# A third set of residual tiles in a hybrid decoder block: x loaded one block ahead, the final norm and its stores spread over the next feed-forward, and tiles shared to make the room

## The reference, cut to what matters

```python
u = rms_norm(h, norm_mix_g) @ w_in                  # 1024 -> 2576
c_val, c_gate, q, k, v, g, gate_lr = split(u)
y_conv = swish(layer_norm(depthwise_conv31(c_val * sigmoid(c_gate))))
y_gla = rms_norm_per_head(gated_linear_attention(q, k, v, gate_lr)) * silu(g)
h = h + concat(y_conv, y_gla) @ w_out               # 1024 -> 1024
h = h + (silu(rms_norm(h) @ w_gate) * (rms_norm(h) @ w_up)) @ w_down   # 2816 wide
out = rms_norm(h, norm_final_g)                     # the meta positions are dropped
```

## Time and profile before

| | us |
|---|---|
| median of 3 runs | 1633.14 |
| the three runs | 1630.55 to 1643.51 |
| the profiled execution's own time | 1627.47 |
| its span on core 4, the slowest | 1625.9 |
| spans of the other cores | 1613.7 to 1622.6 |

### The profile page before, as it was taken

One profiled execution on the slowest core, in us unless ns is written; L12 is line 12 of the kernel. 1 busy time (PEld: TensorE's weight loads), 2 busy tenths in 40 slices (PEclk: granted clock), 3 DMA queues, 4 the chain that ended last, 5 costly groups with the idle time before them and its releaser, 6 DMA issues.

```text
span 1625.9 us, 26606 instructions; the slowest of 8 cores (1613.7 to 1625.9 us)
## 1 busy us (share of the span) xinstructions
PE 1473.5 (91%) x7992; PEld 676.4 (42%) x8066; DVE 810.4 (50%) x1833; ACT 513.8 (32%) x808; POOL 190.8 (12%) x221
## 2 busy tenths in 40 slices
PE   2766999988999979999999988999899999999995
PEld 2333444433444434443444433444344434444442
DVE  5256436644366542754437553566427544475523
ACT  3354243222342224413162222522244131622111
POOL 1050114100040001300040000400013000400000
PEclk9887999999999999999999999999999999999998
DMA  9991899988635875367653776437853676537651
GB/s 211 249 224 52 191 261 200 216 240 222 148 135 165 240 191 159 126 189 242 160 168 123 202 223 161 151 130 218 248 159 125 186 246 161 167 132 193 199 164 65
DMA packets 144171, 294.45 MB, mean 181 GB/s; under 512 B 63264, under 2 KB 80032, under 8 KB 144032
## 3 DMA queue, kind: packets, MB, share of 16 engines
q1 hardware_dynamic: 85008, 253.82, 48.9%
q0 software_dynamic: 7056, 25.23, 9.8%
q10 hardware_dynamic: 51968, 13.70, 5.8%
HBM read 245.70 MB, written 41.94 MB: 177 GB/s over the span
## 4 chain that ended last, share of the span: by engine, by line
PE 71%; DMA 12%; DVE 6%; issue 5%; ACT 2%; ACTq 2%; SPq 2%; POOL 1%; DVEq 0%; POOLq 0%
PE ps L605 48%; PE ps L1146 17%; DMA xT<-xn_tm 5%; DMA wring<-wsc 3%; PE ps L767 2%; DMA wsc<-wring 2%; SPq L714 1%; DVE xn_tm L581 1%; PE ps L674 1%; ACTq L599 1%; ACTq L714 1%; DMA h_2<-xin 1%; DMA gng<-gla_norm_g 1%; DMA wring<-wpack 1%; DVE ftmp L1130 1%
## 5 line engine op out<-in xcount | busy, mean ns | idle before, releaser
L605 PE MATMUL ps<-x2T,wring 128*128 128x512 bf16 x2816 | 639.5, 385 | 38.8 <-DMA wring<-wsc 20.1
L605 PEld LDWEIGHTS ps<-x2T,wring 128*128 128x128 bf16 x2816 | 273.4, 99 | 392.7 <-issue 85.1
L1146 PE MATMUL ps<-wring,actT 128*128 128x512 bf16 x1368 | 312.8, 380 | 5.4 <-DMA wring<-wpack 3.3
L1130 DVE SCALAR_TENSOR_TENSOR ftmp<-ftmp,ps 128x512 f32<-128x512 f32 x176 | 120.1, 685 | 209.2 <-ACT ftmp L1129 206.7
L1129 ACT ACTIVATE ftmp<-ps 128x512 f32<-128x512 f32 x176 | 103.9, 594 | 361.1 <-PE ps L605 255.2
L1146 PEld LDWEIGHTS ps<-wring,actT 128*128 128x128 bf16 x1408 | 136.8, 98 | 163.5 <-issue 5.7
L605 PE MATMUL ps<-xT,wring 128*128 128x512 bf16 x768 | 173.0, 381 | 19.5 <-DMA xT<-xn_tm 10.2
L983 POOL TENSOR_TENSOR Rbd<-S,emid 64x256 bf16<-64x256 f32 x64 | 45.2, 705 | 909.9 <-ACT emid L817 851.3
L1132 DVE SCALAR_TENSOR_TENSOR actT<-ftmp,ps 128x512 bf16<-128x512 f32 x176 | 119.3, 685 | 46.4 <-PE ps L605 39.4
L605 PEld LDWEIGHTS ps<-xT,wring 128*128 128x128 bf16 x768 | 74.5, 98 | 113.7 <-issue 27.7
L605 PE MATMUL ps<-wring,yT 128*128 128x512 bf16 x503 | 116.8, 380 | 1.7 <-DVE sto L551 0.9
(11 more groups left out here) (191 smaller groups left out, 1260.6 us busy)
## 6 DMA issues: line engine op xcount, KB each, us to landing
wring<-wsc SPq DMA_DIRECT2D x336, 512.0 KB, 4.6
wring<-wpack POOLq DMA_DIRECT2D x48, 512.0 KB, 10.6
wsc<-wring SPq DMA_DIRECT2D x48, 512.0 KB, 10.2
rep<-vT SPq DMA_DIRECT2D x240, 67.5 KB, 2.8
h_0<-xin SPq DMA_DIRECT2D x8, 512.0 KB, 9.2
h_1<-xin SPq DMA_DIRECT2D x8, 512.0 KB, 10.2
h_2<-xin SPq DMA_DIRECT2D x8, 512.0 KB, 10.1
h_3<-xin SPq DMA_DIRECT2D x8, 512.0 KB, 10.9
```

The costliest lines, as they stand in the source:

```text
L605: ins = e.matmul(pt_ap, lhsT=lhs(kc), rhs=rhs(kc), start=(kc == 0), stop=(kc == KC - 1))
L1130: P.add("dve", lambda e: e.scalar_tensor_tensor(out=th[:], in0=th[:], scalar=1.0, in1=pg[:], op0=ALU.add, op1=ALU.mult), R=[Bpg, Bth], W=[ ...
L1146: ins = e.matmul(ps[t][:], lhsT=actT[:, j, t * 128:(t + 1) * 128], rhs=wd3[:, j - j0, :], start=(j == 0), stop=(j == NJ - 1))
```

## The change

The residual has three sets of tiles, chosen by `b % 3`. Four things follow from that, and several tiles are given up or shared to make the room.

- The x of block b+2 is loaded during FFN b, one tile behind each of the units j = 14, 16, 18 and 20. It goes into the set from which the result of block b-1 was stored in the same FFN. The x of block 1 is loaded during mixer 0, as soon as `xT` of block 0 is complete.
- The final norm of block b-1 is done during FFN b: one square-and-sum on ScalarE behind each of the units j = 0 to 3, the four row scales together at j = 5, and one scaling on VectorE with its store at j = 5, 7, 9 and 11. The last block keeps its old ending.
- The merged mixer is spread from 0% instead of 10% of the FFN.
- The four silu gates come right after q instead of among the output tiles, in block 0 too, where they stood between v and the conv. They are held in `spb` and `csb`, the decay tiles that k and q have read by then. The two small operations on the decay that followed the state product move into the decay step (`el`, `dec`).
- The conv result and the attention result are written into `xT` instead of `yT`. The attention tiles before their transpose are written into `k_tm` instead of `y_tm`. The low-rank gate's tile is one of `mtmp`, of which there are two instead of three. The starting state of a sequence is kept in memory (`s0_d`) instead of a tile.

```diff
+NH = 3
...
-SPREAD = (0.1, 0.85)
+SPREAD = (0.0, 0.85)
...
+    s0_d = nc.dram_tensor("s0", [128, 256], F32, kind="Internal").ap()
...
-        h = [[sb(f"h{s_}_{t}", [128, D]) for t in range(NT)] for s_ in range(2)]
+        h = [[sb(f"h{s_}_{t}", [128, D]) for t in range(NT)] for s_ in range(NH)]
...
-        yT = sb("yT", [128, KC, T], BF16)
...
-        sg = [sb(f"sg{i}", [128, 512]) for i in range(2)]
-        lrT = sg[0]
...
-        S0 = sb("S0", [128, 2, 128])
+        el = sb("el", [128, 2, NT])
...
-        y_tm = [sb(f"y_tm{i}", [128, 512], BF16) for i in range(2)]
+        y_tm = [k_tm[:, 2 * i:2 * i + 2].rearrange("p a b n -> p (a b n)") for i in range(2)]
...
-        mtmp = [sb(f"mtmp{i}", [128, T]) for i in range(3)]
+        mtmp = [sb(f"mtmp{i}", [128, T]) for i in range(2)]
...
+            blocks = [(s_i * seqlen + b * T, b == 0) for s_i in range(nseq) for b in range(nblk_seq)]
+            nb = len(blocks)
+
+            def load_x(b, t, after):
+                P.add("sp", lambda e: e.dma_start(out=h[b % NH][t][:], in_=xin[blocks[b][0] + t * 128:blocks[b][0] + (t + 1) * 128, :]),
+                      R=after, W=[Bh[b % NH][t]], dkey=f"h{b % NH}_{t}")
+
+            def mixer(bi, first, meta):
+                hs = bi % NH
...
-                    if load:
-                        for t in range(NT):
-                            P.add("sp", lambda e, t=t: e.dma_start(out=h[hs][t][:], in_=xin[row0 + t * 128:row0 + (t + 1) * 128, :]),
-                                  R=[Bact[2 * t + 1]] if bi > 1 else [Bvtm[t]], W=[Bh[hs][t]], dkey=f"h{hs}_{t}")
                     if first and not meta:
-                        P.add("pool", lambda e: e.tensor_copy(out=S[:, s0], in_=S0[:]), R=[BS0], W=[BS[s0]])
+                        P.add("sp", lambda e: e.dma_start(out=S[:, s0].rearrange("p a n -> p (a n)"), in_=s0_d), R=[BS0], W=[BS[s0]], dkey="s0l")
...
+                    lrT, Blr = mtm()
...
+                        if bi == 0 and nb > 1:
+                            load_x(1, t, [BxT[3]])
                         v_tile(lambda kc: xT[:, t, kc, :], [BxT[t]], v_tm[:, t, :], Bvtm[t])
                         if t == NT - 1:
                             wdone(int(bi == 0), 2)
-
-                if bi == 0:
-                    for t in range(NT):
-                        @unit(1.8)
-                        def _(t=t):
-                            gate_tile(t)
...
+                    def decay_main():
+                        decay(spb[:], Bsp, csb[:], Bcs, NT, 0)
+                        em2 = emid[:].rearrange("p (a t) -> p a t", t=NT)
+                        P.add("dve", lambda e: e.tensor_copy(out=el[:], in_=csb[:].rearrange("p a (t n) -> p a t n", n=128)[:, :, :, 127]),
+                              R=Bcs, W=[Bel])
+                        P.add("dve", lambda e: e.tensor_tensor(out=dec[:], in0=em2, in1=el[:], op=ALU.mult), R=[Bemid, Bel], W=[Bdec])
+                    stt["decay"] = decay_main
...
-                        P.add("pool", lambda e: e.tensor_copy(out=S0[:], in_=S[:, s0]), R=[BS[s0]], W=[BS0])
+                        P.add("sp", lambda e: e.dma_start(out=s0_d, in_=S[:, s0].rearrange("p a n -> p (a n)")), R=[BS[s0]], W=[BS0], dkey="s0s")
...
+                for t in range(NT):
+                    @unit(1.8)
+                    def _(t=t):
+                        gate_tile(t)
...
-                    P.add("dve", lambda e: e.scalar_tensor_tensor(out=yT[:, c, :], in0=yth[c], scalar=1.0, in1=y, op0=ALU.add,
-                                                                  op1=ALU.mult), R=[Bysq[c], Bycv[c]], W=[ByTc[c]])
+                    P.add("dve", lambda e: e.scalar_tensor_tensor(out=xT[:, :, c, :], in0=yth[c].rearrange("p (t n) -> p t n", t=NT), scalar=1.0,
+                                                                  in1=y.rearrange("p (t n) -> p t n", t=NT), op0=ALU.add, op1=ALU.mult),
+                          R=[Bysq[c], Bycv[c]], W=BxT)
...
-                    if bi == 0:
-                        return carve(10 + 2 * t, 2, F32), [Bact[10 + 2 * t], Bact[11 + 2 * t]]
-                    return sg[t % 2][:], [Bsg[t % 2]]
+                    return (spb[:, t, :], [Bsp[t]]) if t < 2 else (csb[:, t - 2, :], [Bcs[t - 2]])
...
-                    P.add("act", lambda e: e.activation(out=yT[:, 4:8, t * 128:(t + 1) * 128], in_=ptb, func=AF.Copy,
-                                                        scale=gng[:, 0:1]), R=[Bpt, Bc], W=[ByTg[t]])
+                    P.add("pe", ytr, R=[Bktm[i], Bident], W=[Bpt])
+                    P.add("act", lambda e: e.activation(out=xT[:, t, 4:8, :], in_=ptb, func=AF.Copy,
+                                                        scale=gng[:, 0:1]), R=[Bpt, Bc], W=[BxT[t]])
...
-                    if bi > 0:
-                        gate_tile(0)
                     ln_apply(3)
-
-                if bi > 0:
-                    @unit(1.8)
-                    def _():
-                        gate_tile(1)
...
-                    if t + 2 < NT and bi > 0:
-                        @unit(1.8)
-                        def _(t=t):
-                            gate_tile(t + 2)
...
-                            P.add("pe", mm8(pt[:], lambda kc: yT[:, kc, t * 128:(t + 1) * 128], lambda kc: ws[kc // 4][:, kc % 4, :]),
-                                  R=[B0, B1, ByTg[t]] + ByTc, W=[Bpt])
+                            P.add("pe", mm8(pt[:], lambda kc: xT[:, t, kc, :], lambda kc: ws[kc // 4][:, kc % 4, :]),
+                                  R=[B0, B1, BxT[t]], W=[Bpt])
...
-            def ffn(hs, orow0, last):
+            def stat(b, t):
+                i = nxt("xn", 2)
+                ht, Bht = h[b % NH][t], Bh[b % NH][t]
+                P.add("act", lambda e: e.activation(out=xn_tm[i][:], in_=ht[:], func=AF.Square, accum_out=stf[:, 0, t:t + 1]),
+                      R=[Bht], W=[Bxn[i], Bstf[t]])
+
+            def finish(b, t0, t1, n):
+
+                if n:
+                    newton_row([stf[:, k, t0:t0 + n] for k in range(6)], Bstf[t0:t0 + n], 1.0 / D, RMS_EPS)
+                for t in range(t0, t1):
+                    ht, Bht = h[b % NH][t], Bh[b % NH][t]
+                    P.add("dve", lambda e, t=t, ht=ht: e.scalar_tensor_tensor(
+                        out=ht[:], in0=ht[:], scalar=stf[:, 2, t:t + 1], in1=gfin[:], op0=ALU.mult, op1=ALU.mult),
+                        R=[Bht, Bstf[t], Bgain[id(gfin)]], W=[Bht])
+                    P.add("sp", lambda e, t=t, ht=ht: e.dma_start(out=out[blocks[b][0] + t * 128:blocks[b][0] + (t + 1) * 128, :], in_=ht[:]),
+                          R=[Bht], dkey=f"h{b % NH}_{t}")
+
+            def ffn(b, last):
...
+                        if b > 0 and j < 12:
+                            if j < NT:
+                                stat(b - 1, j)
+                            elif j % 2 == 1:
+                                finish(b - 1, j // 2 - 2, j // 2 - 1, NT if j == 5 else 0)
+                        if b + 2 < nb and j >= 14 and j % 2 == 0:
+                            load_x(b + 2, (j - 14) // 2, [Bact[j]])
...
-                def stat(t):
-                    i = nxt("xn", 2)
-                    P.add("act", lambda e: e.activation(out=xn_tm[i][:], in_=h[hs][t][:], func=AF.Square, accum_out=stf[:, 0, t:t + 1]),
-                          R=[Bh[hs][t]], W=[Bxn[i], Bstf[t]])
...
-                def final():
-                    for t in range(NT):
-                        stat(t)
-                    finish(0, NT)
...
-                        stat(t)
-                        finish(t, t + 1)
-                units.append((19.0, down_last) if last else (0.0, final))
+                        stat(b, t)
+                        finish(b, t, t + 1, 1)
+                if last:
+                    units.append((19.0, down_last))
...
-                f = ffn(b % 2, blocks[b][0], b == nb - 1)
+                f = ffn(b, b == nb - 1)
                 m = mix[b + 1] if b + 1 < nb else []
                 plan += merge(f, m, *SPREAD) if m else [fn for _, fn in f]
```

More of the change, by code:

```diff
@@ L356, in build @@
             P = Prog()
-            Bh = [[Buf(f"h{s_}_{t}") for t in range(NT)] for s_ in range(2)]
+            Bh = [[Buf(f"h{s_}_{t}") for t in range(NT)] for s_ in range(NH)]
             Bxn = [Buf(f"xn{i}") for i in range(3)]
@@ L364, in build @@
             Bx2T = [Buf(f"x2T{t}") for t in range(NT)]
-            ByTc = [Buf(f"yTc{c}") for c in range(4)]
-            ByTg = [Buf(f"yTg{t}") for t in range(NT)]
             BvT = [Buf(f"vT{c}") for c in range(4)]
@@ L373, in build @@
             Bsp = [Buf(f"sp{hp}") for hp in range(2)]
-            Bcs = Buf("cs")
+            Bcs = [Buf(f"cs{hp}") for hp in range(2)]
+            Bel = Buf("el")
             Bmid = Buf("mid")
@@ L378, in build @@
             Bk = [Buf(f"k{hp}") for hp in range(2)]
-            Bktm = Buf("ktm")
+            Bktm = [Buf(f"ktm{i}") for i in range(2)]
             Bvtm = [Buf(f"vtm{t}") for t in range(NT)]
```

(28 more changed lines are left out.)

41 lines of the change are left out of this document (12 added, 29 removed).

## The result

The changed kernel takes 1687.35 us (median of 4 runs, 1678.11 to 1694.09) against 1632.39 for the kernel before: a ratio of 1.0318, 95% interval 1.0241 to 1.0395. It is 3.2% slower. The prediction of 1595 us and its range up to 1625 were wrong. The profiled execution took 1678.11 us, with a span of 1676.2.

A forecast was written before the change was run, and what follows sets the result against it. TensorE, 91% busy, was taken to lose 47.3 us to five waits where stores, loads and transposes come in sequence, plus reduced clock. Terms sum to -37.8: 1589.7 us profiled, 1595 us with the median's 5.7 distance; range 1567 to 1625.

The forecast's parts named there:

- the one on the transposes: Merged blocks: transposes into xT start some 40 us earlier, still in two rounds; one third of 18.4 us gone, 6.1 us.
- What is late next is therefore xT: Merged blocks: once weights are on time, a stall would reappear at the transposes into xT; at worst 14 us more.
- the rest: 0: Merged blocks' earlier gates, shared tiles and state in memory change no TensorE wait, and the ending is unchanged: 0 us.
- Loads and stores, -18: Start of six FFNs: moving eight 512 KB transfers away removes 18 of the 20.1 us waited for weights.
- statistic, -1.3: TensorE's 1.3 us wait for a statistic of x goes, since x lands a whole half-block earlier.
- Final norm -5.4: FFN's first 14 us: moving the final norm out removes two long waits, 5.4 of 7.5 us for FFN products.
- clock -10: Six 14 us windows of reduced clock in the merged blocks lose 13.4 us; 10 of it is gained.
- FFN 0, +3: FFN 0: four loads for block 2 fall into a busy DMA stretch; +3 us, between 0 and 9.6.
- Mixer 0, 0: Mixer 0: moved gates, fewer mtmp buffers and block 1's load give -7 to +9 us; taken as 0.
- The slower one: Rival: final-norm statistics waiting for transposes jam ScalarE's queue in the merged blocks; 1660 to 1680 us, chance 0.10.
- The wait only changes its name: Rival: each gap removed ahead of TensorE's wait for xT lengthens that wait; 1612 to 1630 us, chance 0.18.
- what was to show the prediction wrong: Waits for xT or FFN products over 25 us in total, or mixer 0 or FFN 0 growing by over 9 us.

The follow-up runs named there:

- a3_spread: The changed kernel with only the next mixer's first unit back at a tenth of the FFN's span; ratio 0.992 to the kernel before.
- a2_rep: The changed kernel with the 32 issues of the conv rows ranked behind the weight loads in SyncE's queue; ratio 1.002 to the kernel before.
- c62: The changed kernel with x's Newton step held for the FFN's last additions, conv rows ranked behind weights, block 2's x loaded in mixer 0; ratio 0.978 to the kernel before.
- a1_hold: The changed kernel with the statistics of x waiting for the last additions h + FFN of block b-1; ratio 0.984 to the kernel before.
- a4_alias: Only the freed tiles of the change; two residual sets, loads, final norm and mixer start as in the kernel before; ratio 0.993 to the kernel before.
- a7_latex: The changed kernel with x loaded where the kernel before loads it and the mixer's start back at a tenth; ratio 0.984 to the kernel before.
- c15f: c15 with the final norm and stores back where the kernel before has them, right behind the FFN; ratio 0.982 to the kernel before.
- c125: c15 with the conv rows' issues also ranked behind the weight loads; ratio 0.975 to the kernel before.
- c15: The changed kernel with the statistics of x held back as in a1_hold and block 2's x loaded in mixer 0's output projection; ratio 0.975 to the kernel before.
- a7g: a7_latex with the five small constants loaded ahead of x; ratio 0.978 to the kernel before, median 1590.83 us.
- c26g: c62g with x of block 2 loaded in FFN 0, as in the changed kernel; ratio 0.979 to the kernel before.
- c62g: c62 with the five small constants loaded ahead of x; ratio 0.974 to the kernel before, median 1584.73 us.

## Why the prediction was wrong

**The step that failed** is the one on the transposes: "They start some 40 us earlier in a block, because nothing has to be stored and loaded first." I counted the earlier start as a gain of a third of 18.4 us and asked only for data. I did not ask what else the mixer's instructions would be placed ahead of in queues whose order is fixed. They came ahead of the FFN's additions in VectorE's queue (39.6 us), and brought the rows ahead of the weights in SyncE's (28.7 us). "What is late next is therefore xT" was wrong: the additions to `h` were, and no rival named them. With "the rest: 0" I said that the merged blocks' other changes change no wait. The mixer's spread from 0% had no term at all, and with 0.1 there (a3_spread) no wait for `h` is left.

**Loads and stores, -18; statistic, -1.3.** The waits for weights do go: 0.7 us in a2_rep, 5.6 in c62, and a1_hold has no row of them. But the division was wrong. On the median core, moving the stores and the final norm alone gives 22 us of the merged blocks (a4_alias to a7_latex), moving the loads without them 17 (a4_alias to c15f), and both together 20 to 30 (a4_alias to c125, c62 and c15). On the slowest cores it is 34.6, 21.7 and 36.7 to 39.8. Eight transfers collided; taking four away, the stores or the loads, gave most of it. The Trainium skill's rule that I had weighed ("DMA: Bandwidth & Descriptors", "Queues, rings and completion order"), read as a moved store moving its delay with it, is not borne out by a7_latex: its waits for weights are 14.4 us where a4_alias has 18.3, and 8.1 against 14.0 on the median core.

**Final norm -5.4, transposes -6.1, clock -10.** With both orders repaired, all five of the old waits are 12.6 us in c62 (5.6 weights, 0.8 xT, 6.2 products) where they were 47.3, and the clock's loss is 4.8 where it was 13.4. The merged blocks take 1101.2 us: 41.6 less than before (40.2 on the median core), and the sum of these five terms was 40.8. So the sum was about right for a kernel whose order does not suffer; in the changed one the same stretch is 26.5 longer. Part of that agreement is luck. The two waits that I laid to the transposes fell by 17.6 us where I took 6.1, the one that I laid to the final norm by 1.3 where I took 5.4, and a7g comes as far without the early loads. The freed tiles, which I put at 0, may have a share.

**FFN 0, +3.** Mis-sized: +20.7, and 17.0 on the median core. The wait for `h` at its end is 9.3 of it, and the wait for `Rbd`, which the kernel before does not have there, 11.8. Held statistics take 12.3 off (6.0 on the median core), the moved x of block 2 11.0 (11.7), both 16.8 (14.1). Without the jam the four loads cost 8.5 us (c26g against c62g; 12.6 on the median core), about my upper bound of 9.6, at which none of their bytes is hidden. On the median core the larger part of that is the wait for `Rbd` (8.7 us against 0.2).

**Mixer 0, 0.** On the slowest cores it grew by 3.8, on the median core it fell by 1.5. Its first transposes of x came 6.1 us later (31.81 against 25.75), since the small constant of the last section took 16.4 us to land there; the rest was 2.2 shorter, 4.7 on the median core. a4_alias gained 7.5 there, 6.6 on the median core, so the rest of the change gave some of that back, 5.3 or 1.9; how, no run separates.

**The rivals.** The slower one had nearly the right length, 1660 to 1680 where the runs took 1678 to 1694, but in the wrong queue, so that was luck: ScalarE's statistics do wait for transposes, but held early there they cost nothing (c62). What costs is VectorE's work queued behind them. "The wait only changes its name" was the right kind. Of what was to show the prediction wrong, FFN 0's growth did; the waits for xT and for products, 1.1 us here, were the wrong ones to name. xT's first matmul came 17 us into the FFN, as forecast, and that is where the harm began. Thirteen windows of 14 us had a lowered clock, not two.

## What to carry to other kernels

When data come earlier in a kernel whose order is laid out beforehand, list what the freed instructions will now be placed ahead of, on each engine and in each DMA queue, and what those wait for. A norm that waits for a shared buffer must not stand ahead of the additions that free PSUM. When several transfers collide, price each move alone: the second one may find little left to gain. And where all cores run one program, read a stage on all of them before it is priced; the slowest core of one run and that of another can differ by more than the edit.

## What the runs showed of the hardware that was not expected

**Issues are not free.** 16 issues of 67.5 KB took 11.70 us of SyncE's queue, 0.73 us each, and two such rows stood ahead of seven weight loads. The Trainium skill, "DMA: Bandwidth & Descriptors", "Issuing engines are not separate DMA queues", calls the time to initiate a DMA usually small relative to the DMA. Here 0.73 us is a quarter of the 2.8 us (median, merged blocks) from the issue of such a transfer to its landing, and 16 in a row are four times that; the measurement decides.

**A tiny load can hold up the start.** In a7_latex the last small constant, one column of 128 rows, took 29.60 us to land on the slowest core, and VectorE's queue waited for it ahead of the first norm:

```profile
7.83 29.60 DMA gng<-gla_norm_g
...
37.60 0.17 DVE L506 TENSOR_SCALAR gb<-gb 128x2 f32<-128x2 f32 x1 [21.51 <-DMA gng<-gla_norm_g]
```

Over the eight cores it took 11.0 to 29.6 us, in the kernel before 10.5 to 16.5 (11.03 on the slowest). TensorE's wait behind it was between 9.5 and 28.0 us on the slowest cores of kernels that share the start of the changed one. With the constant ahead of x, VectorE is past it at 10.11 in c62g, and the first transposes of x come at 20.73 to 22.93 us in the three kernels. How much of that lasts until FFN 1 stays open. On the slowest cores most of it is given back: c62g starts FFN 1 at 354.8, and c62, whose first transposes of x came 17 us later, at 357.3. On the median core nothing is: 346.4 against 353.3, for transposes that came 6 us earlier.
